# Two fused transformer blocks in split float32: a 512-column moving operand for the w_out and head products

## What is computed

```python
# end of the first block
h_res = h_res + mix @ w_out[l]          # mix: 2048 channels, w_out 2048 x 2048
out = _rmsnorm(h_res, norm_f_g)

# second block, layer 0 (layer 1: k, v from kv_w, a cumulative forget gate in place of the bias table)
h = rms_norm(x, a_norm[layer])
q, k, v, g = jnp.split(h @ a_w_in[layer], 4, axis=-1)      # 32 heads of 128
o = chunked_relbias_attention(split_heads(q), split_heads(k), split_heads(v), a_rel_bias[layer])
x = x + (o * jax.nn.silu(g)) @ a_w_out[layer]
...
return rms_norm(x, final_norm)
```

## Time and profile before

| | us |
|---|---|
| median of 3 runs | 2743.84 |
| lowest and highest run | 2739.5, 2749.26 |
| profiled execution, first to last instruction | 2741.6 |
| TensorE busy in it | 2632.5 (96%) |
| VectorE busy | 1846.4 (67%) |
| ScalarE busy | 1304.7 (48%) |
| mean granted TensorE clock | 0.981 |

### The profile page before, as it was taken

The page is one execution under the profiler, slowest core; times in us unless marked ns, Lnnn a source line. Parts: engine busy times, 40 slices in busy tenths (PEclk is TensorE's granted clock), DMA queues, the critical chain, the costliest instruction groups (busy, mean ns, idle before and its releaser), DMA issues.

```text
span 2741.6 us, 55845 instructions
## 1 busy us (share of the span) xinstructions
PE 2632.5 (96%) x21178; PEld 2579.7 (94%) x21178; DVE 1846.4 (67%) x2557; ACT 1304.7 (48%) x1930; POOL 339.3 (12%) x371
## 2 busy tenths in 40 slices
PE   7999997688999999999999999999999999999997
PEld 6999994587999999999999999899999999999997
DVE  6888886547766656666665666666666656666664
ACT  5445457344544444544443445544444445444444
POOL 3111015331310000000000000111010100000102
PEclk9999999898999999999999999999999999999998
DMA  6666650007666667666676666567666766666763
GB/s 194 181 161 177 173 153 18 14 4 190 180 165 171 170 175 189 174 173 168 175 187 175 174 168 178 144 174 192 173 179 167 182 186 177 172 183 168 189 177 93
DMA packets 855530, 441.51 MB, mean 161 GB/s; under 512 B 28176, under 2 KB 851472, under 8 KB 855472
## 3 DMA queue, kind: packets, MB, share of 16 engines
q1 hardware_dynamic: 850320, 430.16, 58.8%
q0 software_dynamic: 5152, 10.56, 2.0%
HBM read 437.35 MB, written 3.31 MB: 161 GB/s over the span
## 4 chain that ended last, share of the span: by engine, by line
PE 74%; issue 1%; DVE 1%; DMA 0%; POOL 0%; ACT 0%; DVEq 0%; SPq 0%; POOLq 0%; ACTq 0%
PE bank L235 23%; PE bank L236 23%; PE bank L237 23%; PE bank L1445 1%; PE bank L1425 1%; PE bank L1436 1%; PE bank L1424 1%; PE bank L1430 1%; PE bank L1446 1%; PE bank L1411 0%; DMA rawb<-in_w_out_dram 0%; DVEq L1278 0%; POOL mix L1328 0%; DVE lob L219 0%; DVE mix L1270 0%
## 5 line engine op out<-in xcount | busy, mean ns | idle before, releaser
L235 PE MATMUL bank<-xhi,hib 128*128 128x256 f32 x4352 | 1262.2, 290 | 14.5 <-DVE lob L219 11.4
L237 PE MATMUL bank<-xhi,lob 128*128 128x256 f32 x4352 | 1233.7, 283 | 0.0
L236 PE MATMUL bank<-xlo,hib 128*128 128x256 f32 x4352 | 1233.3, 283 | 0.0
L219 DVE TENSOR_TENSOR lob<-rawb,hib 128x1024 fp32r<-128x1024 f32 x672 | 824.7, 1240 | 458.6 <-ACT hib L212 458.6
L212 ACT ACTIVATE hib<-rawb 128x1024 fp32r<-128x1024 f32 x672 | 698.3, 1056 | 682.1 <-PE bank L237 674.3
L235 PEld LDWEIGHTS bank<-xhi,hib 128*128 128x128 f32 x4352 | 836.7, 192 | 17.8 <-DVE lob L219 15.6
L236 PEld LDWEIGHTS bank<-xlo,hib 128*128 128x128 f32 x4352 | 837.4, 192 | 2.3 <-issue 0.5
L237 PEld LDWEIGHTS bank<-xhi,lob 128*128 128x128 f32 x4352 | 836.2, 192 | 0.0
L235 PE MATMUL bank<-xh,hia 128*128 128x258 f32 (+2 forms) x1040 | 299.9, 288 | 12.2 <-DVE xl L352 12.2
L236 PE MATMUL bank<-xl,hia 128*128 128x258 f32 (+2 forms) x1040 | 296.3, 285 | 0.0
L237 PE MATMUL bank<-xh,loa 128*128 128x258 f32 (+2 forms) x1040 | 295.5, 284 | 0.0
(11 more groups left out here) (300 smaller groups left out, 2429.2 us busy)
## 6 DMA issues: line engine op xcount, KB each, us to landing
rawb<-in_a_w_in_dram SPq DMA_DIRECT2D x256, 512.0 KB, 5.4
rawa<-in_w_in_dram SPq DMA_DIRECT2D x130, 512.0 KB, 5.3
rawb<-in_b_w_in_dram SPq DMA_DIRECT2D x128, 512.0 KB, 5.2
rawb<-in_kv_w_dram SPq DMA_DIRECT2D x128, 512.0 KB, 5.2
rawb<-in_a_w_out_dram SPq DMA_DIRECT2D x64, 512.0 KB, 5.3
rawb<-in_b_w_out_dram SPq DMA_DIRECT2D x64, 512.0 KB, 5.2
rawb<-in_w_out_dram SPq DMA_DIRECT2D x32, 512.0 KB, 5.4
table<-in_rel_dram POOLq DMA_DIRECT2D x32, 128.0 KB, 5.8
```

The costliest lines, as they stand in the source:

```text
L219: nc.vector.tensor_tensor(self.lo[b][:], self.raw[at.u % RAW][:, h * HALF:(h + 1) * HALF], self.hi[b][:].bitcast(F32), ALU.subtract).then_ ...
L235: nc.tensor.matmul(out, self.hi[b][:, w], rhs_hi(k), start=start and k == 0, stop=False)
L236: nc.tensor.matmul(out, self.hi[b][:, w], rhs_lo(k), start=False, stop=False)
L237: last = nc.tensor.matmul(out, self.lo[b][:, w], rhs_hi(k), start=False, stop=stop and k == 7)
```

## The change

In the w_out stage and in the four units of a head, the high and the low part of the activations now lie side by side in one tile (`xx`, 2 x 256 columns per input tile). A step has two matmuls: the high weights on all 512 columns, which fill the whole bank, and the low weights on the 256 high columns, into the bank's first half. The second half of the bank then holds high weights x low activations and has to be added. In w_out VectorE does it with a second add, which waits for the first. In the heads ScalarE copies the second half into `cross` when the unit is computed (semaphore `crossed`), and VectorE adds bank half and copy, waits for that, and multiplies in a second instruction, which then counts `taken`. The products of the first block and the projections are as before.

```diff
+        def unit_wide(self, pe, at, xx, before=({}, {})):
+            out = GB[at.bank()]
...
+                    both = xx[:, 8 * h + k].rearrange("p a t -> p (a t)")
+                    nc.tensor.matmul(out[:], self.hi[b][:, w], both, start=h == 0 and k == 0, stop=False)
+                    last = nc.tensor.matmul(out[:, 0:SEQ], self.lo[b][:, w], xx[:, 8 * h + k, 0], start=False,
+                                            stop=h == 1 and k == 7)
...
-    xhi = [sbuf(ph, f"xhi{i}", [P, KT, SEQ], F32R) for i in range(2)]
-    xlo = [sbuf(ph, f"xlo{i}", [P, KT, SEQ], F32R) for i in range(2)]
+    xx = [sbuf(ph, f"xx{i}", [P, KT, 2, SEQ], F32R) for i in range(2)]
+    xhi = [t[:, :, 0] for t in xx]
+    xlo = [t[:, :, 1] for t in xx]
+    cross = sbuf(ph, "cross", [P, 2, SEQ])
...
-                    st.unit(pe, At(U_WOUT + n, [(i, 4)]), SEQ, xhi[1], xlo[1], before)
+                    st.unit_wide(pe, At(U_WOUT + n, [(i, 4)]), xx[1], before)
...
-                        st.unit(pe, at, SEQ, xhi[src[m]], xlo[src[m]], before)
+                        st.unit_wide(pe, at, xx[src[m]], before)
...
+                    def move_cross(at):
+                        computed(act, at)
+                        a(cross[:, at.bank()], GB[at.bank()][:, SEQ:], ACT.Copy).then_inc(crossed, 1)
                     for at in (q, k, v):
                         for hh in range(2):
                             ahead(split_hi, at, hh)
+                        if at is not v:
+                            move_cross(at)
...
+                    move_cross(v)
                     ahead(split_hi, gg, 0)
...
                     a(pT[:], PT[:, 0:W3], ACT.Copy).then_inc(pt_taken, 1)
+                    move_cross(gg)
...
-                    tt(xraw[:, b], GB[at.bank()][:, 0:SEQ], x1j, ALU.add).then_inc(taken[at.bank()], 1)
+                    tt(xraw[:, b], GB[at.bank()][:, 0:SEQ], x1j, ALU.add).then_inc(summed, 1)
+                    dve.wait_ge(summed, j + 1)
+                    tt(xraw[:, b], GB[at.bank()][:, SEQ:], xraw[:, b], ALU.add).then_inc(taken[at.bank()], 1)
...
+                    def evacuate(m, at, dst):
                         computed(dve, at)
-                        b = GB[at.bank()][:, 0:SEQ]
-                        (stt(dst[:], b, SCALE, inv, ALU.mult, ALU.mult) if dst is qT
-                         else tt(dst[:], b, inv, ALU.mult)).then_inc(taken[at.bank()], 1)
+                        dve.wait_ge(crossed, n * 4 + m + 1)
+                        ch.link(tt(dst[:], GB[at.bank()][:, 0:SEQ], cross[:, at.bank()], ALU.add))
+                        (stt(dst[:], dst[:], SCALE, inv, ALU.mult, ALU.mult) if dst is qT
+                         else tt(dst[:], dst[:], inv, ALU.mult)).then_inc(taken[at.bank()], 1)
```

More of the change, by code:

```diff
@@ L238, in product @@
             if k == 7:
+                last.then_inc(half_used, 1)
+        def unit_wide(self, pe, at, xx, before=({}, {})):
+            out = GB[at.bank()]
+            for h in range(2):
+                b = (2 * at.u + h) % SPL
+                if h == 0:
+                    wait(pe, taken[at.bank()], at.count((at.u - 2) // 2 + 1, 1, 2))
+                pe.wait_ge(lo_ready, at.count(2 * at.u + h + 1, 2))
+                for k in range(8):
+                    if k in before[h]:
+                        before[h][k]()
+                    w = slice(k * P, (k + 1) * P)
+                    both = xx[:, 8 * h + k].rearrange("p a t -> p (a t)")
+                    nc.tensor.matmul(out[:], self.hi[b][:, w], both, start=h == 0 and k == 0, stop=False)
+                    last = nc.tensor.matmul(out[:, 0:SEQ], self.lo[b][:, w], xx[:, 8 * h + k, 0], start=False,
+                                            stop=h == 1 and k == 7)
                 last.then_inc(half_used, 1)
@@ L1194, in _build @@
     PER_HEAD = 4
-    HEAD_CHAIN = 7
+    HEAD_CHAIN = 11
     ph = top.enter_context(ExitStack())
@@ L1199, in _build @@
     x1 = sbuf(ph, "x1", [P, KT, SEQ])
-    xhi = [sbuf(ph, f"xhi{i}", [P, KT, SEQ], F32R) for i in range(2)]
-    xlo = [sbuf(ph, f"xlo{i}", [P, KT, SEQ], F32R) for i in range(2)]
+    xx = [sbuf(ph, f"xx{i}", [P, KT, 2, SEQ], F32R) for i in range(2)]
+    xhi = [t[:, :, 0] for t in xx]
+    xlo = [t[:, :, 1] for t in xx]
+    cross = sbuf(ph, "cross", [P, 2, SEQ])
+    crossed, summed = sem("crossed"), sem("summed")
     oh = sbuf(ph, "oh", [P, GH, SEQ], F32R)
@@ L1637, in head @@
                     q, k, v, gg = (place(layer, g, h, m) for m in range(4))
-                    def evacuate(at, dst):
+                    def evacuate(m, at, dst):
                         computed(dve, at)
-                        b = GB[at.bank()][:, 0:SEQ]
-                        (stt(dst[:], b, SCALE, inv, ALU.mult, ALU.mult) if dst is qT
-                         else tt(dst[:], b, inv, ALU.mult)).then_inc(taken[at.bank()], 1)
-                    for at, dst in ((q, qT), (k, kT)):
+                        dve.wait_ge(crossed, n * 4 + m + 1)
+                        ch.link(tt(dst[:], GB[at.bank()][:, 0:SEQ], cross[:, at.bank()], ALU.add))
+                        (stt(dst[:], dst[:], SCALE, inv, ALU.mult, ALU.mult) if dst is qT
+                         else tt(dst[:], dst[:], inv, ALU.mult)).then_inc(taken[at.bank()], 1)
+                    for m, (at, dst) in enumerate(((q, qT), (k, kT))):
                         ahead(split_lo, at, 0)
                         ahead(split_lo, at, 1)
-                        evacuate(at, dst)
+                        evacuate(m, at, dst)
                     ahead(split_lo, v, 0)
@@ L1669, in head @@
                         ts(pr[:, parts[m]], pr[:, parts[m]], stat[:, 4 + m:5 + m], None, ALU.mult).then_inc(p_ready, 1)
-                    evacuate(v, vT)
+                    evacuate(2, v, vT)
                     ahead(split_lo, gg, 0)
                     ahead(split_lo, gg, 1)
-                    evacuate(gg, gT)
+                    evacuate(3, gg, gT)
                     dve.wait_ge(gate_exp_ready, n + 1)
```

## The result

| | before | changed |
|---|---|---|
| median of the runs, us | 2743.84 | 2778.84 |
| runs, us | 2739.5 to 2749.26 | 2774.26 to 2780.56 |
| span of the profiled execution, us | 2741.6 | 2777.2 |

The ratio is 1.0127, 95% interval 1.0102 to 1.0151: the change makes the kernel 35 us slower. The forecast was 2782.

What follows compares the result with a forecast made beforehand. Bound taken: TensorE's matmul pitch and late operands. Terms +32.3 (42 table-load heads), +1.8 (other 22), +5.4 (projections), -2.0 + 0.5 (w_out) gave +38.0 on 2743.8, so 2781.8 us; range 2750 to 2808.

Steps and rivals of the forecast that it cites:

- s: Time saved per step of w_out and heads by one matmul fewer: 8 ns taken, between 0 and 13.3.
- the upper bound: Matmul pitch in w_out and heads: all 13.3 ns over the columns' time paid once per instruction, so 13.3 ns saved.
- the lower bound: Matmul pitch: excess paid per column, 0.48 ns a column from 256 to 272 columns, so nothing saved per step.
- The float32 row: Plain float32 matmuls, 32 at 217 ns for 213 of streaming: about 4 ns paid per instruction even in long streams.
- step (a): Transposes of v in all 64 heads: TensorE stalls 0.59 us for vT, evacuated 0.87 us later than before.
- (b): Scores in heads without a table load before them: later kT still covered, by 0.1 us, no stall.
- (c): Scores in 42 heads behind a ScalarE table load: 0.39 us later through kT, low part's 0.2 us stall within it.
- (d): First product of a group's projection: ol comes late, 0.68 us times 8 groups, 5.4 us.
- (e): w_out's extra VectorE add of 0.42 + 0.04 us per unit: hidden 16 times, 0.5 us once at the last unit.
- The cover holds: Rival: VectorE reaches kT in time behind table loads, pitch saving whole; 2731 us at the largest saving; chance 0.08.
- Weight path: Rival: weight loads bound TensorE, step 337 ns, 2743 us, no change; chance 0.10.
- The backlog grows: Rival: ScalarE's and VectorE's queues delay value transposes behind table loads another 0.3 us, 13 us more, 2795; chance 0.07.

Runs made afterwards that it cites:

- a_nocross: Changed kernel without ScalarE's copies and VectorE's adds of the second half, in heads and w_out (high x low missing from the result): 2706.56 us, ratio 0.9865.
- a_early: Changed kernel with the first weight split of a unit following a head or projection moved ahead of the next head's table load: 2740.97 us, ratio 0.9992.
- a_lo512: Changed kernel with the low weights too on all 512 columns, so every step has two matmuls of 512: 3169.9 us, one run.
- a_early_turn5: Changed kernel with the first weight split ahead of the table load and the transposes of v after five steps instead of three: 2708.55 us, ratio 0.9883.
- a_early_turn5_sc7: Changed kernel with the early weight split, transposes of v after five steps instead of three, and scores after seven instead of five: 2712.26 us, ratio 0.9883.
- a_turn5: Changed kernel with the transposes of v after five instead of three steps of the gate's first half: 2740.5 us, ratio 0.9991.

## Why the prediction was right, and where it was not

**The pitch.** I took s = 8 between 0 and 13.3. It is 10.3 in the changed kernel and 8.2 to 11.2 in others of the same matmuls (`a_nocross` 351.8, `a_early` 348.8), a mixture of two levels, 346.7 and 353.3. The first is the upper bound, all 13.3 paid per instruction, and `a_lo512` has it with 454. So that argument held for one of the levels and the one for the lower bound fell: the 0.48 ns a column from 256 to 272 does not go on to 512. The float32 row as a price per instruction was weak: it was right that the value lies between, but nothing here shows that 4 ns is the part that counts. (The 32 of that row are also 16 matmuls in the kernel, each recorded as two, and 217 ns is the pitch of one record.) What selects the level of a stretch stays open. It is not TensorE's code alone: w_out has the same instructions in eight of the traces, and its step is 346.7 in five of them and 353.3 in three (`a_nocross`, `a_early_turn5`, `a_early_turn5_sc7`). And each matmul here has a weight load of its own, so no run tells a price per instruction from one per load.

The Trainium skill, "TensorE: Matmul & The Clock Gate", "Back-to-back issue gap": by its 2.5 ns per matmul over the columns, which it gives for isolated matmuls, a step would have gained an estimated 2.5 ns. The runs have 10.3, and 13.7 over the columns at 512; the page's formula is not this kernel's pitch.

**The value turn, step (a).** 0.59 a head was forecast. In the heads without a table load the part from scores to transposes grew by 0.34 while its 14 steps shrank by 0.14: 0.48. In the others it grew by 0.47, of which 0.10 belongs to the late scores below: 0.51. With the 0.06 by which the two transposes stand further apart it is 0.54 to 0.57. So the wait is right in kind and a little smaller than forecast, and `a_turn5` shows that it is a wait for vT that can be covered by two steps.

**The scores, steps (b) and (c).** In the heads without a table load, none, as forecast. In the 42 others they were to come 0.39 us later; they come 0.25 later, and their two first matmuls are 0.10 further apart: 0.35. From the table load to kT's second instruction's end I had 8.65 us and the trace has 8.61. That the load of a matmul which waited starts with it and not a pitch ahead was not in the sum. The low part's wait was forecast as 0.2; it is 0.26 in the head shown and 0.37 in the mean of the 43 behind the first. `a_early` confirms the cause: the queue behind the table load.

**The projection, (d).** 0.68 a group forecast; the wait for ol is 4.3 / 8 = 0.54. **w_out, (e):** hidden, as forecast; the stage and the way to the first scores are 1.7 us shorter (-1.5 forecast).

**The sum.** +32.3 forecast for the 42 heads, +28.7 measured; +1.8 for the other 22, and +0.4 measured (s was larger); projections 5.4, and 2.8 with the shorter steps of the q and k behind them. The interval of the ratio is +28 to +41 us and has the 38 in it. That the median came within 3 us of 2781.8 owes something to the 4.3 us of scatter in the first part of the profiled run: without it the two spans differ by 31 us, where the sum had 38. Terms off by some us each stood on both sides.

**The rivals.** "The cover holds" is out by the trace (0.25 later, not 0.38 earlier), and `a_early` is what it would have looked like: the cover held there only because a step was moved. "Weight path": the step would be 337, and the lower level is 346.7. But 192 columns still take 111.7 ns, 8 under the pitch of 120. If that is a floor, it would bind below some 236 columns (an estimate: (111.7 - 13.3) x 2.4); no run shows a width between. The Trainium skill, "Perfetto Trace Analysis", "Identifying the Most-Contended Engine", would have one judge the distance from the roofline by MFU (the share of the peak rate that the kernel's arithmetic reaches) and by the weight loads' busy share. The latter is 94% before and 84% after, while the time rose by 1.3%: here it fell because a third of the loads went. "The backlog grows": in the head shown VectorE stands idle for 0.21 us before v's evacuation and is released by ScalarE's copy of v, so p was not in its way. It is so in 62 of the 64 heads.

Why there is a ScalarE copy at all: the Trainium skill, "PSUM — Partial Sum Buffer", "Specifications (TRN2)", says that a VectorE instruction takes at most one tensor input from PSUM. No run here shows it; the direct add of the two bank halves was not run.

## What to carry to other kernels

Merging two matmuls that share weights into one of 512 columns saves what is paid per instruction with its weight load, here 8 to 11 ns in a step of 360, 36 us in all where no operand is late. It puts part of the sum into another place, and the add behind it is paid in latency where the next small product waits for the evacuation: 0.87 us, which cost 53 us. Count the slack at every reader of the result first, and move the readers with the change: one number (the transposes after five steps, not three) and one split of weights turned +35 into -35 us.

A faster engine gains only up to the next operand that another queue delivers. In the heads behind a table load 13 us of pitch were lost that way. One instruction of ScalarE moved ahead of the table load gave them back, and the delay of the scores with them: 42 x 0.69 = 29 us. In a fixed order of an engine, look for what stands ahead of the late step without needing to.

## What the runs showed of the hardware that I had not expected

- The step of 512 and 256 columns has two levels, 346.7 and 353.3 ns, with the granted clock at 1.00 in both stretches shown. A level is kept until a small product or a wait interrupts the steps, through some 230 steps of w_out where nothing does, and the same code can have the other level in another kernel's run.
- A matmul of 192 columns with its own 128 x 128 weights has a pitch of 111.7 ns, one of 256 has 120, one of 512 behind another of 512 has 227. Over their columns at 2.4 GHz that is 32, 13 and 14 ns. So neither a price per column nor one per instruction alone fits all three.
- A product that has waited costs more than its wait: the two records of one float32 matmul of 128 columns started 0.213 us apart after a wait and 0.108 to 0.113 without, the transposes 0.165 and 0.108.
